# One core, an encoder block with a mixture of experts: how each expert's results reach the output rows

## The reference

```python
def hierarchical_moe(h, ...):                 # h = rmsnorm(x), 512 rows of 2048
    g_sel = argmax(h @ rg_w + rg_b)           # one of 4 groups per token
    top_v, top_i = top_k(e_logits, 2)         # two of the 8 experts of that group
    gate = g_gate * softmax(top_v)
    ...
    ys = (silu(xb @ w_gate[e]) * (xb @ w_up[e])) @ w_down[e]   # per expert, width 512 inside
    ys = ys * slot_gate[:, None]
    out = segment_sum(ys, slot_tok, num_segments=T)            # back to the tokens' rows
x = x + hierarchical_moe(rmsnorm(x), ...)
```

## Time and profile before

| | |
|---|---|
| median of 3 runs | 1743.7 us |
| profiled execution, its own time | 1739.27 us |
| its span, first to last instruction | 1737.5 us |
| TensorE busy | 1561.2 us (90%) |
| VectorE busy | 622.4 us (36%) |
| ScalarE busy | 333.7 us (19%) |
| GpSimd (POOL) busy | 153.4 us (9%) |
| moved by the DMA engines | 484.37 MB, mean 279 GB/s |
| mean granted TensorE clock | 0.985 |

### The profile page before, as it was taken

The page is one execution under the profiler, slowest core; times in us unless marked ns, Lnnn a source line. Parts: engine busy times, 40 slices in busy tenths (PEclk is TensorE's granted clock), DMA queues, the critical chain, the costliest instruction groups (busy, mean ns, idle before and its releaser), DMA issues.

```text
span 1737.5 us, 18708 instructions
## 1 busy us (share of the span) xinstructions
PE 1561.2 (90%) x7051; PEld 862.8 (50%) x7051; DVE 622.4 (36%) x796; ACT 333.7 (19%) x596; POOL 153.4 (9%) x223
## 2 busy tenths in 40 slices
PE   6999999989999999579998898899889889889997
PEld 6587776768886445434333343333334334333433
DVE  3445656552224223623233133232313213332333
ACT  4222333342221233110101010010010111001010
POOL 1470055410000000000000000000000000000000
PEclk9999999999999999789999999999999999999999
DMA  7432322432216031359999999999999999999994
GB/s 268 121 90 80 92 59 68 156 118 98 97 49 266 1 121 49 145 238 421 422 421 422 421 422 422 421 422 422 422 422 422 422 422 421 422 421 420 419 422 187
DMA packets 114902, 484.37 MB, mean 279 GB/s; under 512 B 9410, under 2 KB 47404, under 8 KB 61868
## 3 DMA queue, kind: packets, MB, share of 16 engines
q1 hardware_dynamic: 110864, 470.84, 67.5%
q0 software_dynamic: 3264, 12.88, 2.0%
q10 hardware_dynamic: 732, 0.07, 0.0%
HBM read 484.81 MB, written 8.39 MB: 284 GB/s over the span
## 4 chain that ended last, share of the span: by engine, by line
PE 64%; DMA 21%; DVE 8%; ACT 3%; issue 2%; ACTq 0%; SPq 0%; DVEq 0%; POOL 0%; POOLq 0%
DMA weight_ring<-in_expert_w_up_dram 21%; PE ps L1878 17%; PE ps L1636 10%; PE ps L1514 8%; PE ps L1906 7%; PE ps L1745 3%; PE ps L1689 3%; PE ps L1855 3%; DVE residual L1396 3%; PE ps L1856 2%; PE ps L1465 2%; PE ps L1476 2%; ACT weight_ring L716 1%; DVE w_in_low L980 1%; PE ps L1456 1%
## 5 line engine op out<-in xcount | busy, mean ns | idle before, releaser
L1878 PE MATMUL ps<-weight_ring,transposed_acts 128*64 128x512 f32 x2048 | 469.0, 595 | 67.3 <-DMA weight_ring<-in_expert_w_up_dram 66.5
L1878 PEld LDWEIGHTS ps<-weight_ring,transposed_acts 128*64 128x64 f32 x2048 | 153.2, 137 | 377.1 <-issue 253.9
L1396 DVE TENSOR_TENSOR residual<-ps,residual 128x1024 f32<-128x1024 f32 x128 | 150.9, 1219 | 262.5 <-PE ps L1856 262.3
L1906 PE MATMUL ps<-weight_ring,transposed_acts 128*64 128x512 f32 x1024 | 226.8, 595 | 19.1 <-DVE transposed_acts L1403 19.1
L1414 DVE SCALAR_TENSOR_TENSOR y_low<-ps,proj_buffer,y_high 64x1024 fp32r<-64x1024 f32 x64 | 82.1, 1283 | 211.3 <-ACT y_high L881 210.3
L1906 PEld LDWEIGHTS ps<-weight_ring,transposed_acts 128*64 128x64 f32 x1024 | 71.8, 137 | 155.4 <-issue 152.5
L881 ACT ACTIVATE y_high<-ps,proj_buffer 64x1024 fp32r<-64x1024 f32 x64 | 70.9, 1108 | 306.2 <-PE ps L1906 305.4
L1855 PE MATMUL ps<-y_high,spread 128*128 128x512 f32 x256 | 113.9, 445 | 14.5 <-DVE residual L1396 10.5
L1514 PE MATMUL ps<-mix_high,w_in_high 128*128 128x512 f32 x288 | 116.6, 405 | 1.3 <-issue 1.3
L873 ACT ACTIVATE transposed_acts<-ps 128x512 f32<-128x512 f32 x32 | 19.1, 598 | 494.4 <-PE ps L1878 494.4
L1514 PE MATMUL ps<-normed_low,w_in_high 128*128 128x512 f32 x288 | 112.3, 390 | 0.0
(11 more groups left out here) (260 smaller groups left out, 1690.9 us busy)
## 6 DMA issues: line engine op xcount, KB each, us to landing
weight_ring<-in_expert_w_gate_dram SPq DMA_DIRECT2D x128, 1024.0 KB, 24.0
weight_ring<-in_expert_w_up_dram SPq DMA_DIRECT2D x128, 1024.0 KB, 25.9
weight_ring<-in_expert_w_down_dram SPq DMA_DIRECT2D x128, 1024.0 KB, 19.0
weight_ring<-in_w_in_dram SPq DMA_DIRECT2D x18, 1024.0 KB, 5.6
weight_ring<-in_w_out_dram SPq DMA_DIRECT2D x16, 1024.0 KB, 5.0
weight_ring<-in_xkv_w_dram SPq DMA_DIRECT2D x8, 1024.0 KB, 6.0
residual<-in_x_dram SPq DMA_DIRECT2D x8, 1024.0 KB, 16.0
weight_ring<-in_xq_w_dram SPq DMA_DIRECT2D x4, 1024.0 KB, 9.5
```

Of the source, the lines that this page charges most:

```text
L1396: v.tensor_tensor(part, ps[:, bank:bank + 2, :].rearrange("p b n -> p (b n)"), part, ALU.add).then_inc(sum_ready if last else part_added, 1)
L1878: ins = mm(ps[side * SLOTS:(side + 1) * SLOTS, 0, :], xsT[:, k, par * SLOTS:(par + 1) * SLOTS], w[:, kk, :], start=(k == 0), stop=(k == KD ...
L1906: ins = mm(ps[half, 4 + n // 2, :], act_t[:, f * SLOTS:(f + 1) * SLOTS], w[:, n * 512:(n + 1) * 512], start=(f == 0), stop=(f == KF - 1), ...
```

## The change

Before the loads of block 1, SP stores X to the output, tile by tile, once each tile has its cross-attention. POOL waits for these four stores before the first transfer of results. After each block ScalarE writes gate times y, unrounded, into `yrows` (lines 0 to 63 for an even block, 64 to 127 for an odd one), and POOL copies the block's 64 token indices into `result_rows` and issues an indirect transfer that adds the rows to the rows of the output in memory. Each such transfer waits until the one before it has landed. The gather of the pair after the next is issued between the two transfers of a pair. ScalarE writes to `yrows` only when the transfer of two blocks earlier has landed. The one-hot matrix, the products with it, the low parts, the adds to X, `last_pair` and the stores at the end are gone.

```diff
+            for t in range(NT):                      # SP, after block 0's loads
+                sp.wait_ge(x_added, 16 + 4 * t + 4)
+                sp.dma_start(out[0, t * P:(t + 1) * P, :], X[:, t, :]).then_inc(stored, 16)
             with sp.Fori(1, NE) as b:
                 load_expert(b, b)
...
-            for t in range(NT):
-                sp.wait_ge(sum_ready, 2 * t + 2)
-                sp.dma_start(out[0, t * P:(t + 1) * P, :], X[:, t, :]).then_inc(stored, 16)
...
-            g.iota(tramp, pattern=[[1, S]], base=0, channel_multiplier=0,
-                   allow_small_or_imprecise_dtypes=True).then_inc(tramp_ready, 1)
...
+            def scatter(pair, half, done, ready, known):
+                rows = slice(half * SLOTS, (half + 1) * SLOTS)
+                wait_past(pool, scattered, done)
+                pool.wait_ge(y_act, ready)
+                g.tensor_copy(outcols[:, half:half + 1], tokf[0:SLOTS, ds(pair * 2 + half, 1)]).then_inc(ids_copied, 1)
+                pool.wait_ge(table_ready, 1)
+                pool.wait_ge(ids_copied, known)
+                g.indirect_dma_start(out=out[0], out_offset=bass.IndirectOffsetOnAxis(ap=outcols[:, half:half + 1], axis=0),
+                                     in_=yrows[rows].rearrange("p n m -> p (n m)"), in_offset=None,
+                                     bounds_check=S - 1, oob_is_err=False,
+                                     compute_op=ALU.add).then_inc(scattered, 16)
...
+                scatter(pair, 0, *first)             # results(pair, fetch)
+                if fetch:
+                    pool.wait_ge(xs_turned, turned_)
+                    g.tensor_copy(cols[:, 0:1], tokf[:, ds(pair * 2 + 4, 1)]).then_inc(idx_copied, 1)
...
+                    g.indirect_dma_start(out=xs, out_offset=None, in_=hn_dram, ...).then_inc(gathered, 16)
+                scatter(pair, 1, *second)
...
             gather(0)
             gather(1)
-            with pool.Fori(2, NE // 2 + 1) as it:
-                gather(it)
+            pool.wait_ge(stored, 16 * NT)
+            results(0, True)
+            with pool.Fori(1, NE // 2 - 1) as it:
+                results(it, True)
+            results(NE // 2 - 1, False)
             pool.wait_ge(gathered, 16 * (NE // 2 + 1))
+            pool.wait_ge(scattered, 16 * NE)
...
                 act.wait_ge(used, b * 12 + (UE + 12))
+                if not isinstance(b, int):
+                    act.wait_ge(scattered, act.to_reg(b * 16 - 16))
                 for side in range(2):
                     rows = slice(side * SLOTS, (side + 1) * SLOTS)
-                    a.activation(y_hi[par * SLOTS:(par + 1) * SLOTS, side:4:2, :], ps[rows, 4:6, :], ACT.Copy,
+                    a.activation(yrows[par * SLOTS:(par + 1) * SLOTS, side:4:2, :], ps[rows, 4:6, :], ACT.Copy,
                                  scale=gate[rows, ds(b, 1)]).then_inc(y_act, 1)
...
-                    v.tensor_tensor(part, ps[:, bank:bank + 2, :].rearrange("p b n -> p (b n)"), part,
-                                    ALU.add).then_inc(sum_ready if last else part_added, 1)
...
-                        mm(ps[:, bank, :], spread[:, t * P:(t + 1) * P], y_hi[:, cols_, :], start=True, stop=False)
-                        ins = mm(ps[:, bank, :], spread[:, t * P:(t + 1) * P], y_lo[:, cols_, :], start=False, stop=True)
...
-                wait_past(pe, y_dve, b * 2)
+                wait_past(pe, y_act, b * 2)
```

More of the change, by code:

```diff
@@ new lines, in results @@
+            def results(pair, fetch):
+                first = [reg(v) for v in (pair * 32, pair * 4 + 2, pair * 2 + 1)]
+                second = [reg(v) for v in (pair * 32 + 16, pair * 4 + 4, pair * 2 + 2)]
+                if fetch:
+                    turned_, copied = reg(pair * 4 + 8), reg(pair + 3)
+                scatter(pair, 0, *first)
+                if fetch:
+                    pool.wait_ge(xs_turned, turned_)
+                    g.tensor_copy(cols[:, 0:1], tokf[:, ds(pair * 2 + 4, 1)]).then_inc(idx_copied, 1)
+                    pool.wait_ge(table_ready, 1)
+                    pool.wait_ge(idx_copied, copied)
+                    g.indirect_dma_start(out=xs, out_offset=None, in_=hn_dram,
+                                         in_offset=bass.IndirectOffsetOnAxis(ap=cols[:, 0:1], axis=0),
+                                         bounds_check=S - 1, oob_is_err=False).then_inc(gathered, 16)
+                scatter(pair, 1, *second)
@@ L578, in _ @@
             with pool.If(more > 0):
-                with pool.Fori(NE // 2 + 1, NBLK // 2 + 1) as it:
-                    gather(it)
+                with pool.Fori(NE // 2, NBLK // 2) as it:
+                    gather(it + 1)
+                    results(it, False)
                 pool.wait_ge(gathered, 16 * (NBLK // 2 + 1))
+                pool.wait_ge(scattered, 16 * NBLK)
         @block.scalar
@@ L1433, in _ @@
                     block_dve(b + 1, 1, it)
[L1434 to L1438, removed]
         @block.tensor
@@ L1841, in expert_landed @@
                 pe.wait_ge(landed[s], b * 16 + 16 * (early_loads[s] + 1))
-            def spread_parts(before, half, last=False):
-                for i in range(4 * half, 4 * half + 4):
-                    t = i // 2
-                    if i >= 2:
-                        if last:
-                            pe.wait_ge(sum_ready, i - 1)
-                        else:
-                            pe.wait_ge(part_added, before + (i - 1))
-                    for n in range(2):
-                        bank, cols_ = (6, 2)[i % 2] + n, 2 * (i % 2) + n
-                        mm(ps[:, bank, :], spread[:, t * P:(t + 1) * P], y_hi[:, cols_, :], start=True, stop=False)
-                        ins = mm(ps[:, bank, :], spread[:, t * P:(t + 1) * P], y_lo[:, cols_, :], start=False, stop=True)
-                    ins.then_inc(part_done, 1)
[L1859 to L1863, removed]
             def block_pe(b, par, pair):
@@ L1882, in block_pe @@
                 if par == 1:
-                    if pair is not None:
-                        pe.wait_ge(part_added, pair * 8)
                     turn_rows(1 if pair is None else pair + 1)
-                behind = par == 0 and pair is not None
-                if behind:
-                    pe.wait_ge(y_dve, b * 2)
-                    pe.wait_ge(spread_ready, pair)
-                    spread_parts(pair * 8 - 8, 0)
                 pe.wait_ge(gu_copied, b + 1)
@@ L1922, in _ @@
                     block_pe(b + 1, 1, it)
-                last_pair(NBLK)
-            with pe.If(more < 1):
-                last_pair(NE)
 _INS = ['x', 'mem', 'mix_norm_g', 'w_in', 'q_norm_g', 'k_norm_g', 'sink_logits', 'pool_w', 'pool_scale', 'w_out',
```

40 lines of the change are left out of this document (6 added, 34 removed).

## The result

| | before | after |
|---|---|---|
| median of the runs | 1745.17 us (4 runs) | 1785.09 us (4 runs, 1782.21 to 1786.24) |
| ratio | | 1.0228, 95% interval 1.0201 to 1.0255 |
| profiled execution, its span | 1739.27, 1737.5 us | 1786.24, 1784.4 us |
| TensorE busy | 1561.2 us | 1502.5 us |
| VectorE busy | 622.4 us | 382.8 us |

What follows compares the result with a forecast made beforehand. Weight loads were taken to bound the expert stage, with added rows on the slowest DMA engine paid on top: 1739.3 + 76.9 for added rows - 15 for the tail = 1801 us, range 1752 to 1842.

Steps and rivals of the forecast that it cites:

- The bound: Expert stage: weight loads set the pace, 59.8 us per pair; removing TensorE's spreading products gives nothing inside the stage.
- The price: Added row's time on its DMA engine: 0.62 us, twice a plain row's 0.31; bounds 0.31 and 0.93 us.
- The rows on the slowest engine: Result transfers in the expert stage: four filled rows on one engine in each of 31 transfers, +76.9 us.
- one half block on eight engines: Rival on result transfers: each half block uses eight engines, 96 rows, 59 us, giving 1784; rows-otherwise rivals together 0.22.
- The tail: After the last down products: shorter end saves 12 us, TensorE nearer to the loads 3 us more; 15 us together.
- The clock: TensorE in the expert stage: at half clock it would set the pace, some 350 us in all; chance 2 in 100.
- Pairs of 65 to 68 us: Sign in the expert stage: time between POOL's index copies per pair of experts, in place of 61 to 62 us.
- Weights at 375 GB/s: Sign in the expert stage: the rate of weight loads falls to about 375 GB/s.
- Queue 0's share near 8%: Sign in the expert stage: share of the queue of gathers and result transfers rises from 2% to some 8%.
- TensorE's waits at 300 us: Sign in the expert stage: TensorE's waits for weights grow from 66 us to some 300.
- The span's end under 10 us after the last scaling: Sign at the kernel's end: the span ends under 10 us after ScalarE's last scaling.
- the first gather came later than 746 us: Counter-sign at the expert stage's start: early stores were counted as zero cost; a gather after 746 us would refute the forecast.

Runs made afterwards that it cites:

- e1: Changed kernel with the 32 transfers of results left out, index copies kept; 1724.5 us, ratio 0.9888 to the kernel before.
- e2: Changed kernel with the transfers writing their rows over those of the output, not adding; 1759.7 us, stage 994.1 us.
- e3: Changed kernel with result rows of even and odd blocks both on lines 0 to 63, in two buffers; 1785.5 us.
- e4: Changed kernel with an expert's slots filled in the order 0, 1, 32, 33, then 2, 3, 34, 35 and so on; 1824.7 us.
- e5: Changed kernel with slots filled in an order that spreads filled rows over the DMA engines; 1773.8 us.
- e6: Kernel before the change, with slots filled in an order that spreads filled rows over the DMA engines; ratio 0.9965, median 1737.8 us.
- e8: Kernel before the change, with the four early residual stores added ahead of block 1's loads, end stores kept; 1745.4 us, ratio 1.0003.

## Why the prediction was right, and which term was mis-sized

**The bound.** Right. The stage ran at the pace of the weight loads and still does; the products' removal gave nothing there (e1, 0.7 us).

**The price.** Right: 0.62 us was taken for an added row, twice a plain one; the page gives 0.66 with the small packets, single packets 0.63, and e2 removes half of the stage's loss. The rule of the Trainium skill that was weighed against it ("Collectives: The Full Stack", the section on the bandwidth ceiling) says the same of a copy that reads two sources. Here the trace agrees, 0.66 to 0.33.

**The rows on the slowest engine.** This is **the term that was mis-sized**. The prediction said: "if 64 rows go to 16 engines in groups of four, as the gathers' fours suggest, one engine always gets four filled rows ... I take four. Of 32 transfers 31 lie in the loaded stage: 31 x 4 x 0.62 = +76.9 us". Measured were 47.8 us, 2.5 rows per transfer at that price. The fours were right for the gathers of 128 rows. In a transfer of 64 the fullest engine gets two of the first 32 slots and, only if the expert has more than 32 rows, two of the rest. That gives four per pair of small experts, eight per pair of large ones, and the pairs grew by 2.3 and 4.5 us; this rule gave e3, e4, e5 and e6 within 5 us each before they ran, and the length of the transfers in the packet records bears it out (under e4). The reading "one half block on eight engines" gives nearly the same count, which is why that rival's 1784 us came so close, and e3 excludes it.

The size fits less well than the rule. By it engine 0 has 89 added and 77 gathered rows in the stage, 56 + 24 = 80 us above bare weights; in e1 the fullest has 84 gathered rows, 26 us. The difference, 54 us, is 6 more than the 47.8 measured. The pairs of large experts are 0.5 us short of it each (66.6 against 62.1 + 5.0). In e4, where the count is nearly the same for every pair, it fits to 2 us. The packet records hold no engine, so which one takes the rows from 33 on was not measured singly, and where the 6 us went stays open.

**The tail.** "12 us" and "3 us more" were 7.1 together. Up to the landing the steps are near what was worked out: 2.6 us to the index copy, 1.0 to the issue and 4.5 us to land, with 21 rows added, against 5.4 expected. Missed was what stands behind it on POOL: reading the branch value and the drain, 6.0 us from landing to the end. The three us of a TensorE nearer to the loads did not come either (stage of e1: 0.7 us less). Between a block's last gate and up products and its first down products lie the copy, the transposes, silu and the product with it, 1759.7 to 1763.18 us in the last block; at 2.49 us a chunk the down chunks have by then partly landed (an estimate from that pace), and the 32 products run in one go of 7.09 us as before.

**The total.** It fits better than its terms do, and that is luck in part: the stage was taken 30 us too dear (76.9 against 47.2) and the tail 8 us too cheap, and the sum started from an execution 6 us under the median.

**The clock.** It fell more often, for 0.97 of full over 820 to 1690 us in place of 1.00, and the gate and up products took 627 ns a record (595 before). Hidden, as far as e1 can show it: there the clock was 0.98 and the pairs were those of before.

**What was named as a sign.** Pairs of 65 to 68 us: only six of fourteen, those that add the results of two large experts. Weights at 375 GB/s: 390 MB per 1001 us, 390 GB/s. Both follow from the count. Queue 0's share near 8% in the loaded stage: it is 5.9%, and here the prediction's own arithmetic was off, since the share counts all rows and not those of the fullest engine; 1003 rows at 0.62 us are under 4% of 16 engines' time, beside the 2% that it had. TensorE's waits at 300 us: 148, of which slower products account for some, since those of the gate and up stages were busy 66 us longer (484.6 against 418.8); the rest was not followed up. The span's end under 10 us after the last scaling: 1784.4 - 1772.74 = 11.7, by the drain. Of what would have made the forecast wrong, the pairs did not stay at 62 us and ScalarE did not wait, but the first gather came later than 746 us, at 752.36; by e8 the stores are not shown to be the cause.

## What to carry to other kernels

Where a stage runs at the pace of its loads, work taken from the compute engines is worth nothing in the stage (0.7 us here), and each row that a DMA engine must carry besides is paid in full; a row added in memory was paid twice here, 0.63 against 0.31 us. Count such rows on the fullest engine, not in the mean: the order in which slots are filled was worth 40 us one way and 11 us the other with not a byte moved more. And look at what stands behind the last transfer on the engine that issued it.

## What was not expected of the hardware

The added rows' 8 KB are counted once in the bytes moved (492.76 - 484.37 = 8.39 MB), and their second read not at all among the memory reads, so the rate on the page falls (403 to 420 GB/s) with the DMA engines as busy as before. The page's memory writes grow by twice the rows' bytes (8.39 to 25.17 MB), with the add and also without it in e2. The engine's share of time shows the cost, its rate does not. GpSimd's closing drain took 4.6 us just behind a landed transfer of results, 6.9 us beside one that had not landed, and 2.2 us in e1, 70 us after its last transfer. It is not the distance alone: in the kernel before it took 2.2 us too, at 1657.5 us, about 1 us after POOL had seen its last gather land, one without a filled row. What sets it was not settled. And a transfer of 64 rows is dealt to the DMA engines otherwise than one of 128 (e4), whatever lines its rows stand on (e3).
